# Opening stage of a one-core fp32 decoder layer: q, k and v blocks taken in pairs with seven quarter products, memory items moved ahead of them, and four residual additions moved in GpSimd's order at the end

## The chip, the cores and the metric

The kernel runs on one core of one Trainium2 chip, in one launch. The metric is device time in microseconds (us). Engines are named as in the profile: PE is the tensor engine's matmul (PEld its weight load), DVE the vector engine, ACT the scalar engine, POOL is GpSimd, SP is the engine that issues the DMAs.

## What is computed

One layer of a hybrid decoder for 1024 tokens of width 1024: a norm, one wide input projection, three token mixers (stick-breaking attention, an SSD scan, cross-attention to 256 memory tokens), their merge, and an MLP. The part that is changed is this:

```python
u = rms_norm(h, norm_mix_pre[layer])
proj = u @ w_in[layer]                      # 12320 columns
sb_qkv, z, xbc_raw, dt_raw, mem_q, gate_logits = jnp.split(proj, SPLIT_POINTS, axis=-1)
q, k, v = jnp.split(sb_qkv, 3, axis=-1)     # 1024 columns each
...
kv = rms_norm(mem, norm_mem) @ w_mem_kv     # 256 tokens, 2048 columns
...
ff = jnp.square(jax.nn.relu(u @ w_up[layer])) @ w_down[layer]
h = h + rms_norm(ff, norm_mlp_post[layer])
```

## The kernel before, in words

Every fp32 product is made of three passes. Each operand is rounded to fp32r ("hi") and the rest of it is kept ("lo"); `split3` names the passes hi*hi, hi*lo, lo*hi. So a block of 128 output columns for 1024 tokens, with an inner length of 1024, is 2 halves x 8 k-steps x 3 passes = 48 matmuls of 512 columns, and a memory item (128 columns, 256 memory tokens) is 24 matmuls of 256 columns.

`front` is the opening stage. Each of ten tiles (eight of x, two of mem) is squared and summed on ACT (`root_of`), scaled on DVE (`invert`), turned on PE (`turn`), multiplied by the gain on DVE from PSUM (`scale_turned`, result in `scaled`), rounded on ACT (`round_u`), and its rest taken on DVE (`rest_of_u`). Two weight blocks (b = 0, 1) are multiplied while the tiles come in, by `piece`, two tiles at a time. Then PE makes the projection of dt (48 matmuls, L464) and works through `ITEMS`: 22 further blocks of q (b < 8), k (b < 16) and v (b < 24), with the 16 memory items set between them. Weights come through a ring of three slots; POOL rounds them (L393) and takes their rest (L399). ACT evacuates each product, DVE takes the rest for q and k. Between blocks stand the small steps for dt, its running sums and their tables (L486 to L502, L547 to L559, L602 to L627).

`stick_breaking` follows in the same block of programs, with no barrier between. Its SP part begins with `early_loads`, called from inside `front`. Its PE program works in events. Event i first asks for score i, which needs ACT's `beta` of event i-1, then runs a share of filling matmuls (`project`, L822: x, z and mem_q blocks, 48 matmuls per block) and turns the weights of event i-2. ACT and DVE go through the same events in order. Block m = 0 is evacuated in halves (`evacuate`, L903), the first of them in event 1.

The MLP at the end, `mix_and_mlp`, already makes its up-projection (L2610) by seven quarter products for a pair of blocks: 7 x 4 k-steps x 3 passes = 84 matmuls instead of 96. The down-projection takes 112 items of 12 matmuls (L2709). For each item POOL makes a weight difference (L2500), ACT rounds weight and activation (L2874, L2882) and DVE takes both rests (L3207, L3212). POOL's list also holds four residual additions (L2565), each of which waits for DVE's `scale` (L3238) of an output tile.

Of the kernel before, what the change touches and what calls it, by code (L numbers as in the profile page):

```python
# [80 lines left out]
class FrontSignals:  # L81
    u_split: Any
    kv_out: Any
    hi_out: Any
    qk_stored: Any
    v_stored: Any
# [149 lines left out]
def front(nc, ctx, a, proj, qk, kv, decay, table, dt_out, xh, xl, consts):  # L236

    def sb(n, shape, dt=F32):
        return ctx.enter_context(nc.sbuf_tensor(f"fr_{n}", shape, dt))
# [4 lines left out]
    N_BLOCKS, N_QK, N_KV = Z0, V0, 2 * KB  # L244
    FIRST_KV = 5
    SLOTS = 3
    ITEMS = [("in", b) for b in range(FIRST_KV + 1)]
    for m in range(N_KV):
        ITEMS += [("kv", m), ("in", FIRST_KV + 1 + m)]
    ITEMS += [("in", b) for b in range(FIRST_KV + 1 + N_KV, N_BLOCKS)]  # L250
    TILES = TB + MB

    w_raw = sb("w", [P, SLOTS, D])
    w_hi, w_lo = sb("wh", [P, SLOTS, KB, P], F32R), sb("wl", [P, SLOTS, KB, P], F32R)
    v_tile = sb("v", [P, 2, S])
    memh, meml = sb("memh", [P, KB, M], F32R), sb("meml", [P, KB, M], F32R)
    x_tile, u, square = sb("x", [P, 4, D]), sb("u", [P, 2, D]), sb("sq", [P, D])
    scaled = sb("scaled", [P, 2, D])
    stats, gains, warm = sb("stats", [P, 3, TILES]), sb("gains", [P, 2, KB]), sb("warm", [P, 1])
    hi_tile, lo_tile = sb("hi", [P, 2, S], F32R), sb("lo", [P, 2, S], F32R)  # L260
    wd, wdh, wdl = sb("wd", [P, KB, 32]), sb("wdh", [P, KB, 32], F32R), sb("wdl", [P, KB, 32], F32R)
    bias_row, a_row = sb("bias", [P, 32]), sb("a", [P, 32])
    raw, capped, soft = (sb(n, [P, TB, 32]) for n in ("dtraw", "dtcap", "dtsoft"))
    ps = ctx.enter_context(nc.psum_tensor("fr_ps", [P, 2, S], F32))
    ps_misc = ctx.enter_context(nc.psum_tensor("fr_psm", [P, 4, HALF], F32))
    turned = [ps_misc[:, 2 * s:2 * s + 2].rearrange("p a n -> p (a n)") for s in range(2)]
    ps_dt = ps_misc[:, 0, 0:TB * 32].rearrange("p (t c) -> p t c", t=TB)
    ps_dtT = ps_misc[0:32, 1:3].rearrange("p a n -> p (a n)")
    ps_turned_sums = ps_dtT
    ps_cs = ps_misc[:, 3].rearrange("p (a n) -> p a n", a=2)  # L270
    ps_kv = [ps_misc[:, bank, 0:M] for bank in (0, 3)]
    dtT = sb("dtT", [32, S])
    da_out, sums = sb("da", [P, TB, SSD_HEADS]), sb("cs", [P, TB * SSD_HEADS])
    tables = sb("tables", [P, 3, TB * SSD_HEADS])
    sumsT, grownT = sb("csT", [32, S]), sb("grownT", [32, S])
    kv_tile = sb("kvout", [P, 2, M])
# [3253 lines left out]
```

## Time and profile before

| what | value |
|---|---|
| device time, median of 3 | 2713.86 us (2713.6 to 2715.26) |
| device time of the profiled execution | 2712.84 us |
| its span | 2711.1 us |
| granted clock, mean | 0.99 |
| PE busy | 2626.2 us, 97% of the span |
| DVE, ACT, POOL busy | 1707.7, 1124.3, 1384.2 us |
| last matmul of `front` starts | 356.10 us into the span |

PE is busy in 97% of the span, so what counts is the number of its matmuls and the few places where it stands still. Busy time of PE is modelled for pipelined matmuls: one matmul lasts longer than the distance to the next, so distances between starts are the better measure.

### The profile page before, as it was taken

Reading aid. Unit: us, or ns where it says so; the run is one execution under the profiler, and the core shown is the slowest. Engines: PE = TensorE matmul, PEld = TensorE weight load, DVE = VectorE, ACT = ScalarE, POOL = GpSimd, SP = SyncE. Lnnn points to the kernel's source line nnn. Section 1 sums busy time; section 2 is a strip of 40 time slices with the busy share of each in tenths; the row PEclk is TensorE's granted clock in tenths of the full one; section 3 lists DMA queues with packets and bytes.
Section 4 is the critical chain, followed back from the end, with each engine's and each line's share of the span. In section 5 each row is a group of like instructions: output and inputs, shape, how many; then the busy total and the mean of one; then the engine's idle time right before and its main releaser. Section 6 shows DMA issues by size and latency. Waiting matters only on the chain. (4 is left out here: it accounts for less than half of the span.)

```text
span 2711.1 us, 35282 instructions
## 1 busy us (share of the span) xinstructions
PE 2626.2 (97%) x12884; PEld 2199.2 (81%) x12884; DVE 1707.7 (63%) x1899; ACT 1124.3 (41%) x2001; POOL 1384.2 (51%) x831
## 2 busy tenths in 40 slices
PE   7999999999999999799999999999999999999998
PEld 6888888888888888688888777878887788888886
DVE  6100046776777677488888756663358877768567
ACT  4111034444444444466666554443144222244443
POOL 3466634545554554378887832545500666535224
PEclk9999999999999999899999999999999999999999
DMA  4344424243433332366676653444331344376573
GB/s 150 140 169 160 149 95 123 93 132 109 114 112 104 114 94 94 119 183 193 197 208 202 218 207 128 156 147 140 132 124 55 144 163 156 135 241 211 203 252 142
DMA packets 205994, 407.32 MB, mean 150 GB/s; under 512 B 19585, under 2 KB 100097, under 8 KB 205825
## 3 DMA queue, kind: packets, MB, share of 16 engines
q1 hardware_dynamic: 205824, 405.08, 45.3%
q8 instruction: 105, 1.72, 0.3%
q14 instruction: 65, 0.52, 0.1%
HBM read 286.91 MB, written 118.10 MB: 149 GB/s over the span
## 5 line engine op out<-in xcount | busy, mean ns | idle before, releaser
L989 POOL TENSOR_TENSOR sb_beta<-sb_beta,sb_rest 128x128 f32<-128x128 f32 (+7 forms) x128 | 164.1, 1282 | 388.9 <-DVE sb_rest L1049 388.9
L822 PE MATMUL sb_psg<-uh,sb_wl 128*128 128x512 f32 x768 | 309.9, 403 | 0.0
L822 PE MATMUL sb_psg<-ul,sb_wh 128*128 128x512 f32 x768 | 305.2, 397 | 0.0
L822 PE MATMUL sb_psg<-uh,sb_wh 128*128 128x512 f32 x768 | 303.7, 395 | 0.0
L2709 PE MATMUL ff_ps<-ff_mh,ff_total 128*128 128x512 f32 x896 | 279.3, 392 | 5.6 <-DVE ff_total L3212 5.6
L1049 DVE TENSOR_TENSOR_SCAN sb_rest<-sb_rest 128x128 f32<-128x128 f32 (+7 forms) x128 | 185.2, 1447 | 151.1 <-ACT sb_rest L938 150.9
L2709 PEld LDWEIGHTS ff_ps<-ff_mh,ff_total 128*128 128x128 f32 x896 | 169.6, 189 | 42.7 <-issue 7.1
L1854 PE MATMUL first_ps<-uh,mg_wh 128*128 128x512 f32 x480 | 192.8, 402 | 7.4 <-DVE ul L2059 4.9
L1854 PE MATMUL first_ps<-uh,mg_wl 128*128 128x512 f32 x480 | 187.7, 391 | 0.0
L1854 PE MATMUL first_ps<-ul,mg_wh 128*128 128x512 f32 x480 | 187.6, 391 | 0.0
L2709 PE MATMUL ff_ps<-ff_ml,ff_total 128*128 128x512 f32 x448 | 175.5, 392 | 0.0
L822 PEld LDWEIGHTS sb_psg<-ul,sb_wh 128*128 128x128 f32 x768 | 144.7, 188 | 29.7
L822 PEld LDWEIGHTS sb_psg<-uh,sb_wl 128*128 128x128 f32 x768 | 145.1, 189 | 25.9
L822 PEld LDWEIGHTS sb_psg<-uh,sb_wh 128*128 128x128 f32 x768 | 145.3, 189 | 24.8
L901 ACT ACTIVATE sb_wth<-sb_pst 128x512 fp32r<-128x512 f32 (+1 forms) x192 | 87.3, 489 | 187.6 <-PE sb_pst L807 187.6
L426 PE MATMUL fr_ps<-uh,fr_wh 128*128 128x512 f32 (+1 forms) x416 | 157.5, 379 | 6.7 <-DVE ul L583 6.7
L1341 PE MATMUL first_ps<-uh,sg_wh 128*128 128x512 f32 x384 | 154.2, 402 | 7.9 <-ACT ssd_out L1406 7.0
L426 PE MATMUL fr_ps<-ul,fr_wh 128*128 128x512 f32 (+1 forms) x416 | 156.2, 375 | 0.0
L426 PE MATMUL fr_ps<-uh,fr_wl 128*128 128x512 f32 (+1 forms) x416 | 155.9, 375 | 0.0
L1341 PE MATMUL first_ps<-ul,sg_wh 128*128 128x512 f32 x384 | 150.4, 392 | 0.0
L1341 PE MATMUL first_ps<-uh,sg_wl 128*128 128x512 f32 x384 | 150.4, 392 | 0.0
L997 DVE TENSOR_TENSOR sb_wtl<-sb_pst,sb_wth 128x512 fp32r<-128x512 f32 (+1 forms) x192 | 99.7, 547 | 74.2 <-ACT sb_wth L901 74.2
(378 smaller groups left out, 7120.0 us busy)
## 6 DMA issues: line engine op xcount, KB each, us to landing
sb_w<-in_w_in SPq DMA_DIRECT2D x48, 512.0 KB, 4.5
scratch_proj<-sb_out SPq DMA_DIRECT2D x48, 512.0 KB, 2.9
ff_w<-in_w_down SPq DMA_DIRECT2D x96, 256.0 KB, 3.6
sb_k<-scratch_qk SPq DMA_DIRECT2D x64, 256.0 KB, 6.3
ssd_arow<-scratch_decay SPq DMA_DIRECT2D x32, 512.0 KB, 5.6
mg_gate<-scratch_proj SPq DMA_DIRECT2D x32, 512.0 KB, 3.6
ff_w<-in_w_up SPq DMA_DIRECT2D x32, 512.0 KB, 3.8
mg_w<-in_w_branch SPq DMA_DIRECT2D x30, 512.0 KB, 4.3
```

What stands on the lines that cost most here:

```text
L426: last = nc.tensor.matmul(ps[:, b % 2, cols], l[:, s, k], r[:, k, cols], start=(k == 0 and j == 0), stop=(k == KB - 1 and j == 2))
L822: last = nc.tensor.matmul(ps_g[:, h], l[:, s, k], r[:, k, h * HALF:(h + 1) * HALF], start=(k == 0 and j == 0), stop=(k == KB - 1 and j == 2))
L901: nc.scalar.activation(out, src, ACT.Copy).then_inc(hi_done, 1)
L989: nc.gpsimd.tensor_tensor(beta[:, i % 3, 0:cols], beta[:, i % 3, 0:cols], rest[:, i % 3, 0:cols], ALU.mult).then_inc(weighted, 1)
L997: nc.vector.tensor_tensor(out, src, hi, ALU.subtract).then_inc(lo_done, 1)
L1049: nc.vector.tensor_tensor_scan(kept, kept, kept, 1.0, ALU.mult, ALU.bypass).then_inc(scanned, 1)
L1341: last = nc.tensor.matmul(ps_g[:, h], l[:, s, k], r[:, k, h * HALF:(h + 1) * HALF], start=(k == 0 and j == 0), stop=(k == KB - 1 and j == 2))
L1854: last = nc.tensor.matmul(ps[:, s, cols], l[:, k], r[:, k, cols], start=(k == 0 and j == 0), stop=(k == KB - 1 and j == 2))
L2709: done = nc.tensor.matmul(down_bank(p, local), l[:, columns(local)], r, start=(begins and c == 0 and j == 0), stop=(c == PAIRS - 1 and j = ...
```

## The change

`front` is rewritten. Blocks 0 and 1 stay as they are. The 16 memory items come next, one after another, and their weights are rounded by ACT and finished by DVE instead of by POOL. Then blocks 2 to 23 come as 11 pairs. A pair is treated as a 2x2 matrix of quarters (two row blocks, two halves of k) times a 2x2 matrix of u (two halves of k, two halves of the tokens), and is made by seven products of 12 matmuls (`p1`, `p5`, `p2`, `p6`, `p7`, `p4`, `p3`) with sums of weight quarters made by POOL (`weight_sums`) and sums of quarters of u (T1 to T4) made once by POOL and split by ACT and DVE during the memory items. T1 takes the place of the quarter B12 of u in `xh`, `xl`; B12 is stored to DRAM (`kept`) and loaded back at the end by `load_kept`. DVE adds up the outputs (`c11` to `c12`). `early_loads` has the new loads in it, and the two tiles of the last pair are stored after it. ACT's first `evacuate` in `stick_breaking` waits for all stores of `front` (`before.outs`). In the MLP the four residual additions stand at other items of POOL's list.

```diff
+        def near_sums(i):
+            j = i - TB // 2
+            pool.wait_ge(gained, i + 1)
+            pool.wait_ge(raw_kept, TB)
+            x = by_block(scaled[:, i % 2])
+            minus(T1_raw[:, :, columns(j)], x[:, LOWER], B11_raw[:, :, columns(j)]).then_inc(t_near, 1)
+            minus(T3_raw[:, :, columns(j)], x[:, UPPER], x[:, LOWER]).then_inc(t_near, 1)
...
-        for n in range(2, len(ITEMS)):
-            round_item(n)
-            rest_of_item(n)
+        for i in range(TB // 2, TB):
+            near_sums(i)
+        pool.wait_ge(t_near, TB)
+        nc.gpsimd.tensor_tensor(T2_raw, T3_raw, B11_raw, ALU.add).then_inc(t_far, 1)
+        pool.wait_ge(t_far, 1)
+        minus(T4_raw, T2_raw, B21_raw).then_inc(t_far, 1)
+        for c in range(PAIRS):
+            weight_sums(c)
...
+        def product(p, c, factor, moving):
+            for k in range(Q):
+                for j, (l, r) in enumerate(split3(*zip(factor, moving))):
+                    done = nc.tensor.matmul(bank(p, c), l[:, k * P:(k + 1) * P], r[:, k],
+                                            start=(k == 0 and j == 0), stop=(k == Q - 1 and j == 2))
+            done.then_inc(p_done[p], 1)
...
+        for m in range(N_KV):
+            product_of_memory(m)
+            if m == 2:
...
+            if m == 7:
                 pe.wait_ge(dt_dve, 5)
                 da_all = da_out[:].rearrange("p c h -> p (c h)")
...
+        for m in range(N_KV):
+            if 1 <= m <= 4:
+                round_t(m)
+            evacuate_kv(m)
+            if m + 3 < N_KV:
+                round_kv(m + 3)
+            if m == 5:
                 act.wait_ge(dt_dve, 2)
...
+            if m == 6:
                 dve.wait_ge(dt_act, 3)
...
     def early_loads(sp):
-        sp.wait_ge(before.u_split, TILES)
+        for signal, count in before.qk_outs:
+            sp.wait_ge(signal, count)
+        sp.wait_ge(before.p_done[6], before.pairs)
         load(sp, 0)
-        load_qk(sp, 0, 0)
+        load_q(sp, 0, 0)
         load(sp, 1)
+        sp.wait_ge(before.p_done[4], before.pairs)
+        load_k(sp, 0, 0)
+        before.load_kept(sp)
...
                 if m < 2:
-                    stored_before, blocks = ((before.kv_stored, KV_BLOCKS), (before.v_stored, V_BLOCKS))[m]
-                    for x in range(2):
-                        act.wait_ge(stored_before[x], 16 * blocks // 2)
+                    for signal, count in before.outs:
+                        act.wait_ge(signal, count)
...
+            else:
+                pool.wait_ge(before.p_done[7], before.pairs)
...
             for t in range(TB // 2):
-                if n == 6 * PAIRS + 5 + 3 * t:
+                if n == min(6 * PAIRS + 11 + 2 * t, N_DOWN - 1):
                     pool.wait_ge(scaled_done, t + 1)
```

POOL in the opening stage. Before, behind the two rests of the first weight blocks and the split of dt's weights, its list went on with the rounding and the rest of weight item 2, and so on for 38 items:

```order
L399 TENSOR_TENSOR fr_wl<-fr_w,fr_wh 128x1024 x2
L405 CAST fr_wdh<-fr_wd 128x256
L407 TENSOR_TENSOR fr_wdl<-fr_wd,fr_wdh 128x256
L393 TENSOR_TENSOR fr_wh<-fr_w,small 128x1024
L399 TENSOR_TENSOR fr_wl<-fr_w,fr_wh 128x1024
```

Now, at the same place, come the sums for the last four tiles of x (`fr_f_hi` is `scaled`, `fr_f_t` the raw T and B quarters), one pair of rows for each tile, and then the two long ones:

```order
L498 TENSOR_TENSOR fr_fl<-fr_w,fr_fh 128x1024 x2
L532 CAST fr_wdh<-fr_wd 128x256
L534 TENSOR_TENSOR fr_wdl<-fr_wd,fr_wdh 128x256
L494 TENSOR_TENSOR fr_f_t<-fr_f_hi,fr_f_t 128x4x128
L494 TENSOR_TENSOR fr_f_t<-fr_f_hi 128x4x128
...
L538 TENSOR_TENSOR fr_f_t<-fr_f_t 128x2048
L494 TENSOR_TENSOR fr_f_t<-fr_f_t 128x2048
L516 TENSOR_TENSOR fr_f_sums<-fr_w 128x512
```

No weight splitting is left in POOL's list; eight short and two long sums of u stand there, then four sums per pair.

SP at the hand-over from `front` to `stick_breaking`. Before, the early loads of `sb_` tiles followed the last memory item's store, while three v blocks were still to be made:

```order
L337 DMA scratch_kv<-fr_kvout 128x256
L742 DMA sb_w<-in_w_in 128x1024
L730 DMA sb_q<-scratch_qk 64x1024
L732 DMA sb_k<-scratch_qk 64x1024 x2
L730 DMA sb_q<-scratch_qk 64x1024
L732 DMA sb_k<-scratch_qk 64x1024 x2
L742 DMA sb_w<-in_w_in 128x1024
```

Now they begin after the sixth product of the last pair, and the store of the last two v blocks (L451, 512 KB each) is the last row:

```order
L1168 DMA sb_w<-in_w_in 128x1024
L1150 DMA sb_q<-scratch_qk 64x1024 x2
L1168 DMA sb_w<-in_w_in 128x1024
L1157 DMA sb_k<-scratch_qk 64x1024 x4
L1029 DMA uh<-scratch_kept 128x4x512
L1029 DMA ul<-scratch_kept 128x4x512
...
L1150 DMA sb_q<-scratch_qk 64x1024 x2
L1157 DMA sb_k<-scratch_qk 64x1024 x4
L1162 DMA sb_vraw<-scratch_proj 128x1024
L451 DMA scratch_proj<-fr_f_tiles 128x1024 x2
```

Two 1 MB loads have come in (`uh`, `ul`), and seventeen transfers now stand ahead of the last stores of v, besides two small ones (conv weights).

POOL at the end of the MLP, last group of items. `ff_f_vh` are the output tiles. Before:

```order
L2500 TENSOR_TENSOR ff_f_vl<-ff_w,ff_f_vl 128x512 x6
L2565 TENSOR_TENSOR ff_f_vh<-ff_f_vh,ff_f_near 128x1024
L2500 TENSOR_TENSOR ff_f_vl<-ff_w,ff_f_vl 128x512 x3
L2565 TENSOR_TENSOR ff_f_vh<-ff_f_vh,ff_f_near 128x1024
L2500 TENSOR_TENSOR ff_f_vl<-ff_w,ff_f_vl 128x512 x3
```

Now:

```order
L2948 TENSOR_TENSOR ff_f_vl<-ff_w,ff_f_vl 128x512 x12
L3013 TENSOR_TENSOR ff_f_vh<-ff_f_vh,ff_f_near 128x1024
L2948 TENSOR_TENSOR ff_f_vl<-ff_w,ff_f_vl 128x512 x2
L3013 TENSOR_TENSOR ff_f_vh<-ff_f_vh,ff_f_near 128x1024
L2948 TENSOR_TENSOR ff_f_vl<-ff_w,ff_f_vl 128x512 x2
L3013 TENSOR_TENSOR ff_f_vh<-ff_f_vh,ff_f_near 128x1024 x2
```

Twelve weight differences instead of six stand ahead of the first addition, and no difference is left behind the third.

## Rows read from the trace of the kernel before

**Rows 1.** A window of the opening stage: busy us of each engine, clock, DMA share, GB/s.

```profile
150.00:200.00 50.00, 50.00 (x267) 43.34 (x266) 4.90 (x4) 5.41 (x8) 32.86 (x16) 1.00 0.46 159
```

**Rows 2.** Timeline of PE in the opening stage: start, duration, line, tiles.

```profile
262.04 0.39 PE L426 MATMUL fr_ps<-uh,fr_wl 128*128 128x512 f32 x1
...
265.44 0.39 PE L426 MATMUL fr_ps<-uh,fr_wl 128*128 128x512 f32 x1
265.67 0.28 PE L442 MATMUL fr_psm<-fr_memh,fr_wh 128*128 128x256 f32 x1
...
268.42 0.28 PE L442 MATMUL fr_psm<-fr_memh,fr_wl 128*128 128x256 f32 x1
```

**Rows 3.** Window of the MLP's up-projection, columns as in rows 1.

```profile
2160.00:2180.00 20.00, 20.00 (x90) 16.57 (x89) 16.73 (x21) 4.60 (x7) 13.55 (x10) 1.00 0.48 178
```

**Rows 4.** Timeline of DVE, one tile of the opening norm.

```profile
46.56 1.22 DVE L577 TENSOR_TENSOR fr_scaled<-fr_psm,fr_gains 128x1024 f32<-128x1024 f32 x1
48.91 1.23 DVE L583 TENSOR_TENSOR ul<-fr_scaled,uh 128x1024 fp32r<-128x1024 f32 x1 [1.13 <-ACT uh L515]
...
50.24 0.76 DVE L568 TENSOR_SCALAR fr_u<-fr_x,fr_stats 128x1024 f32<-128x1024 f32 x1
50.91 1.22 DVE L577 TENSOR_TENSOR fr_scaled<-fr_psm,fr_gains 128x1024 f32<-128x1024 f32 x1
```

**Rows 5.** Timeline, a POOL and a DVE instruction at the same time.

```profile
56.32 2.42 POOL L399 TENSOR_TENSOR fr_wl<-fr_w,fr_wh 128x1024 fp32r<-128x1024 f32 x1
...
56.75 3.07 DVE L583 TENSOR_TENSOR fr_meml<-fr_scaled,fr_memh 128x1024 fp32r<-128x1024 f32 x1 [1.13 <-ACT fr_memh L515]
```

**Rows 6.** The tile of the dt projection: ns min/median/max, first and last start.

```profile
L464 PE MATMUL fr_psm<-uh,fr_wdh x16: 387/390/397, 56.9 to 67.2; 128*32 128x512 f32 x16
```

**Rows 7.** Timeline of POOL, a difference of 512 columns.

```profile
2213.07 1.29 POOL L2509 TENSOR_TENSOR ff_f_total<-ff_w 128x512 f32<-128x512 f32 x1 [0.72 <-DVE ff_total L3143]
```

**Rows 8.** Groups of ACT by line: busy, mean ns, idle before.

```profile
L515 ACT ACTIVATE uh<-fr_scaled 128x1024 fp32r<-128x1024 f32 x8 | 8.5, 1057 | 15.6 <-DVE fr_scaled L577 15.6
L524 ACT ACTIVATE fr_kvout<-fr_psm 128x256 f32<-128x256 f32 x16 | 6.1, 384 | 28.6 <-PE fr_psm L442 28.6
```

**Rows 9.** Timeline of ACT, the step for dt.

```profile
83.65 0.42 ACT L549 ACTIVATE fr_dtsoft<-fr_dtcap 128x256 f32<-128x256 f32 x1 [2.34 <-DVE fr_dtcap L611]
...
85.91 1.28 ACT L552 ACT_TABLE_LOAD   x1
87.20 0.23 ACT L552 ACTIVATE fr_a<-fr_a 128x32 f32<-128x32 f32 x1
```

**Rows 10.** DMA issues of the page: count, KB each, median us to landing.

```profile
sb_w<-in_w_in SPq DMA_DIRECT2D x48, 512.0 KB, 4.5
```

**Rows 11.** Timeline at the hand-over: PE, then ACT.

```profile
356.32 0.39 PE L822 MATMUL sb_psg<-uh,sb_wh 128*128 128x512 f32 x1
...
366.34 0.60 ACT L918 ACTIVATE sb_padded<-sb_psg 128x512 f32<-128x512 f32 x1 [3.52 <-PE sb_psg L822]
...
367.21 0.50 ACT L942 ACTIVATE sb_beta<-sb_psz 128x384 f32<-128x384 f32 x1
...
370.95 0.60 ACT L938 ACTIVATE sb_rest<-sb_psz 128x512 f32<-128x512 f32 x1 [2.15 <-PE sb_psz L843]
```

**Rows 12.** Windows around the hand-over, columns as in rows 1.

```profile
324.00:346.00 22.00, 22.00 (x99) 18.20 (x98) 1.37 (x4) 1.63 (x3) 10.01 (x5) 1.00 1.03 264
...
360.00:364.00 4.00, 2.87 (x8) 2.44 (x9) 1.85 (x2) 1.73 (x5) 2.30 (x2) 0.65 0.33 117
```

**Rows 13.** Waits from 2560 us on: us in total, times, longest.

```profile
PE ff_ps L2709 <- DVE ff_total L3212: 5.6, 4, 2.6
```

**Rows 14.** Timeline of PE and POOL in the last items.

```profile
2670.34 0.47 PE L2709 MATMUL ff_ps<-ff_mh,ff_total 128*128 128x512 f32 x1 [0.67 <-DVE ff_total L3212]
...
2675.90 2.73 POOL L2565 TENSOR_TENSOR ff_f_vh<-ff_f_vh,ff_f_near 128x1024 f32<-128x1024 f32 x1 [1.16 <-DVE ff_f_vh L3238]
...
2703.40 0.39 PE L2709 MATMUL ff_ps<-ff_mh,ff_total 128*128 128x512 f32 x1
```

More of the change, by code:

```diff
@@ L81 @@
 class FrontSignals:
[L82 to L86, printed above, removed]
+    pairs: Any
+    p_done: Any
+    raw_used: Any
+    bank_free: Any
+    qk_outs: Any
+    outs: Any
+    stored_at: Any
+    load_kept: Any
+    b12_back: Any
     kv_stored: Any
@@ L233, in product, with front @@
     return last
-def front(nc, ctx, a, proj, qk, kv, decay, table, dt_out, xh, xl, consts):
-    def sb(n, shape, dt=F32):
-        return ctx.enter_context(nc.sbuf_tensor(f"fr_{n}", shape, dt))
+def front(nc, ctx, a, proj, qk, kv, decay, table, dt_out, kept, xh, xl, consts):
     def sem(n):
         return nc.alloc_semaphore(f"fr_{n}")
[L244 to L276, printed above, removed]
@@ new lines, in front, with small @@
+    with ExitStack() as plain_view:
+        plain = layout(plain_view, "f_", F32)
+    held = layout(ctx, "", F32R)
+    def small(n, shape, dt=F32):
+        return ctx.enter_context(nc.sbuf_tensor(f"fr_{n}", shape, dt))
+    raw, fh, fl, hi_tiles = held["w"], held["fh"], held["fl"], held["hi"]
+    tiles, tiles_low = plain["tiles"], held["tiles"]
+    p1_kept = held["p1"]
+    sums = [plain["sums"][:, x // 2, (x % 2) * HALF:(x % 2 + 1) * HALF] for x in range(4)]
+    first_low = held["sums"]
@@ new lines, in front @@
+    back_hi, back_lo = ([held["back"][:, 2 * x + y] for x in range(BACK)] for y in range(2))
+    x_tile = plain["back"][:, 0:8].rearrange("p (s a) n -> p s (a n)", a=2)
+    square = plain["back"][:, 8:10].rearrange("p a n -> p (a n)")
+    third_hi, third_lo = (held["back"][:, x:x + 2].rearrange("p a n -> p (a n)") for x in (6, 8))
+    u, scaled = plain["sums"], plain["hi"]
+    memh, meml = (held["tiles"][:, x:x + 2].rearrange("p a n -> p (a n)").rearrange("p (k m) -> p k m", k=KB) for x in (0, 2))
@@ L420, in turn, with piece @@
             last.then_inc(turned_done, 1)
-        def piece(n, cols):
-            s, b = n % SLOTS, ITEMS[n][1]
+        def piece(b, cols):
+            half = cols.start // HALF
+            out = acc[:, 2 * b + half, cols.start - half * HALF:cols.stop - half * HALF]
             for k in range(KB):
-                for j, (l, r) in enumerate(split3((w_hi, xh), (w_lo, xl))):
-                    last = nc.tensor.matmul(ps[:, b % 2, cols], l[:, s, k], r[:, k, cols],
+                for j, (l, r) in enumerate(split3((fh, xh), (fl, xl))):
+                    last = nc.tensor.matmul(out, l[:, b, k * P:(k + 1) * P], r[:, k, cols],
@@ new lines, in vector @@
+            if m == 14:
+                rest_of_front(0)
+        for which in (S1, S2, S3, A22, S4):
+            rest_of_back(which, 0)
+        for c in range(PAIRS):
+            more = c + 1 < PAIRS
+            if c and is_split(c - 1):
+                for row in range(2):
+                    lo_of_tile(c - 1, row)
+            if more:
+                rest_of_front(c + 1)
+                rest_of_back(S1, c + 1)
+            c11(c)
+            make_u2(c)
+            if more:
+                rest_of_back(S2, c + 1)
+            make_u3(c)
+            make_u4(c)
+            c22(c)
+            if more:
+                rest_of_back(S3, c + 1)
+            c21(c)
+            if more:
+                rest_of_back(A22, c + 1)
+            c12(c)
+            if more:
+                rest_of_back(S4, c + 1)
@@ L730, in load_qk, with load_k @@
             sp.dma_start(q_both[to, a].bitcast(F32), qk[half, p + Q0, rows]).then_inc(qk_loaded[a], 16)
+    def load_k(sp, p, a):
+        rows = slice(64 * a, 64 * a + 64)
+        for half in range(2):
+            to = slice(64 * half, 64 * half + 64)
             for part in range(2):
```

654 lines of the change are left out of this document (493 added, 161 removed).

## The prediction

> **What bounds the kernel now.** I read the windows first. In the opening stage PE is busy 50.00 of 50 us at full clock, while DVE and ACT work about a tenth of the time [rows 1]. So from the dt projection to the end of `front` only PE's own work counts, and every matmul taken away is time, as long as what feeds PE keeps up. The price of a matmul comes from distances between starts: 15 matmuls of 512 columns lie between 262.04 and 265.44, or 0.2267 us each; 23 matmuls of 256 columns lie between 265.67 and 268.42, or 0.12 us each [rows 2]. In the norm of the tiles ahead of it the tiles follow each other at a fixed distance of 50.91 - 46.56 = 4.35 us. That is a loop through two engines: DVE scales (1.22), ACT rounds (DVE waits 1.13 for it), DVE takes the rest (1.23), then makes the next tile's `fr_u` (0.76, behind a reciprocal) and scales again [rows 4]. At the end of the MLP PE waits four times for DVE, 5.6 us in all [rows 13].
>
> **Term 1, the matmuls.** Eleven pairs at 84 instead of 96 matmuls are 132 fewer. At 0.2267 us that is **-29.9 us**. Whether PE can run at that pace in this form shows in the MLP's up-projection, which has the same seven products per pair: 20.00 of 20 us busy at full clock, DVE at 16.73 and POOL at 13.55 [rows 3]. A pair takes 84 x 0.2267 = 19.0 us there and here. The new pairs ask for less: ACT about 7 us (copies of 512 and 1024 columns at 0.6 and 1.06 [rows 8, 11]), DVE some 12 rests and sums of 512 columns and three rests of 1024 at 1.23 [rows 4], about 11 us, POOL four sums at 1.29 [rows 7], 5 us. That work I cost at nothing; it lies beside the pair's 19.0 us of PE, and without that cover the longest of it, DVE's, would add up to 11 us per pair.
>
> **Term 2, the norm of the tiles.** POOL gets two sums of 512 columns per tile for the last four x tiles, then two of 2048. DVE and POOL can't both work on SBUF operands: POOL's instruction runs from 56.32 to 58.74, and DVE's rest, ready at 56.75, ends at 59.82, its own 1.1 us behind POOL's end [rows 5]. The first short sum (1.29) hides behind ACT's 1.13. The second falls between DVE's rest and its next scaling, so the loop goes from 4.35 to about 5.6 us for three distances: +3.8. The extra copies on ACT in the early tiles cost little (+0.8 at the first piece), and POOL no longer splits item 2 there (-1.3). So the scaling of tile 7, before at 46.56 [rows 4], comes at about 49.9. One loop of 5.6 on, tile 8 is scaled at 55.5 to 56.7, and at the same moment POOL begins its first sum of 2048 columns, four times 1.29 less overheads, say 4.9, until 60.4. ACT has rounded tile 8 at 57.8; DVE's rest of it waits for POOL and ends at 61.6, and the scaling of tile 9 at 62.8. The dt projection waits for that one and begins at 62.9 instead of 56.8 [rows 6]: **+6.1 us** (low 2.5, if the short sums hide wholly; high 9, if the second long sum gets in ahead of DVE as well). The rest of tile 9, held by the second sum until 67.5, is hidden behind the dt projection's 10.9 us.
>
> **Term 3, the memory items in a row.** Sixteen items of 24 matmuls take 2.88 us each, as before. But each now also asks ACT for a rounding (1.06) and an evacuation (0.38) [rows 8], and DVE for a rest (1.23). During items 1 to 4 ACT and DVE also split T1 to T4, 2048 columns each: twice the 1.06 and twice the 1.23 for 1024, about 2.1 us on ACT and 2.4 on DVE. So ACT has 3.5 and DVE 3.6 us of work in 2.88; three items of lead take up most of it, about +0.9. The larger piece is dt. ACT's step from the first exponential to the last takes 83.65 to 87.43, and a table load like the one at 85.91 (1.28 us) goes ahead of it, so some 5 us [rows 9]. Behind it in ACT's list stand evacuation 6 and rounding 9, and only behind the rest of item 9 does DVE make `fr_da`, for which PE waits after item 7. From the end of product 5: evacuation and rounding 1.4, the wait for `capped` and the step to about 8.2, evacuation 6 and rounding 9 to 9.6, rest 9 (1.23) and three short DVE instructions for dt (together 0.9) to 12.1. PE arrives 2 x 2.88 after product 5, plus 0.9 that item 7 is late, at 6.7: PE stands for **5.4 us**. Before, a whole block of 10.9 us covered this step, and nothing was ahead of it on DVE. After a stop of 2 us the clock was granted at 0.65 over four us [rows 12], a loss of 1.4; for this one I take 2. Two smaller waits (for the running sums after item 10, 0.3; for the last evacuation ahead of pair 0, 0.5) make the term **+9.1 us** (low 1, if the dt step's table load is done in advance and ACT runs ahead; high 13).
>
> **Term 4, the hand-over.** Let T be the start of the last pair; its products end every 2.72 us, the seventh at T+19.0. The first `sb_w` is asked for at T+10.9 and lands 4.5 us later [rows 10]; POOL's rest takes up to 2.42 [rows 5] and its rounding somewhat less, together 4.3, so PE can begin at T+19.7: +0.7. Then comes the queue. Before, the same loads were asked for 30 us earlier. The transfers from `sb_w` to the stores of v are 5 x 0.52 MB (two weights, one v, two stores), 12 x 0.26 MB (q and k) and 2 x 1.05 MB (B12), 7.9 MB. The early loads ran at 264 GB/s with the DMA engines full [rows 12], so 7.9 MB take 30 us, and the stores, asked for last, are down at T+42. Score 0 needs its k (fifth to eighth transfer), at about T+24 instead of T+22.1: +1.9. ACT's first evacuation comes 10.0 us after the first matmul of the stage [rows 11], here at T+31.5, and stands for the stores until T+42. Behind it in ACT's list are the sigmoids of event 2, and PE's score 3 waits for those. Before, ACT had finished them at 367.7 and stood 2.15 us of the 3.2 until 370.95 for score 3 [rows 11]; between the two I take 2.6 us that PE has in hand: 10.5 - 2.6 = 7.9. The clock after the stop: 2. Sum **+12.5 us** (low 1, high 16).
>
> Here a rule gives another result. By the Trainium skill (DMA: Bandwidth & Descriptors, "Where 436 GB/s comes from") it is the memory side that binds such transfers, at about 358 GB/s per core. An estimate by that page: 7.9 MB in 22 us, the stores down at T+35, k early enough, and a term of about 4 us. The row with 264 GB/s, more than half of it the same q and k loads, decides for me.
>
> The early loads and the stores may also not wait for one another as I assume; both ways the result is the first rival below.
>
> **Term 5, the end of the MLP.** Now POOL waits for `scale` at item 101 and stands; the sums behind come late, each addition takes 2.7 us in which DVE waits [rows 14]. From the first late item at 2670.34 to the last matmul at 2703.40 lie nine items of 12 matmuls, which at 0.2267 take 24.5 us; PE used 33.1, and it had waited 0.7 before the first. With 5.6 us of waits [rows 13] the rest is slow clock. After the change twelve sums stand ahead of the first addition, and DVE needs per item 2 x 0.6 and POOL 1.25, plus 0.6 for `scale`, 3.1 us against 2.72 for a few items, within a lead of five. **-9 us** (-5 if one addition still bites; no gain beyond 33.1 + 0.7 - 24.5 = 9.3 is there). The outputs 0 to 3 are then added some 5 us before PE ends, so their stores don't delay the last ones.
>
> **Sum.** -29.9 + 6.1 + 9.1 + 12.5 - 9.0 = -11.2 us, against a profiled execution of 2712.84 us (span 2711.1): 2701.6. The median of the runs is 1.0 above the profiled one, so **2702.6 us**. 0.2% of the time, 5.4 us, is about what a measurement can tell from no change.
>
> **Rivals.**
> - The hand-over is nearly free, because the queue drains at the faster rate or the stores don't stand behind the loads: by rows, if the 7.9 MB take no longer than the 20.5 us from T+11 to ACT's need at T+31.5 (385 GB/s), only the 0.7 and at most the 1.9 are left, and the time is 2692.7. For it: the two loads of B12 and the stores fill all partitions, unlike q and k (64 rows each). Against it: the DMA engines stood at a share of 1.03 for 22 us in the early loads [rows 12]. Chance 0.2.
> - The memory items cost more: each of the four splits of T pushes ACT and DVE further behind, and the stop for dt costs the full clock penalty twice; term 3 at 15 to 17 and term 2 at 9 give 2709 to 2713, no change that can be told. ACT's 3.5 and DVE's 3.6 us against 2.88 speak for it, the lead of three slots against it. Chance 0.13.
> - Slower: the pairs starve. SP's list has the stores of pair c, which wait for ACT's and DVE's split of its tiles in the next pair, ahead of the next weight loads, and POOL's sums wait for both weights of a pair. I find some 9 us in hand for the last factor of a pair. If a round took that and 2.8 us more over ten pairs (28 us), the time would be 2730; from 0.6 us per pair on the change is no longer faster by more than 0.2%, from 1.7 on it is slower by more than that. Against it: the same order of products with busier engines loses nothing in the MLP [rows 3]. Chance 0.1.
> - The forecast as it stands, 2697 to 2707: 0.47. The rest, 0.1, is the forecast with term 5 or term 1 smaller by some us.
>
> **How the numbers follow.** The range 2690 to 2711 takes in the free hand-over and most of the second rival, and leaves out the starving pairs. Faster by over 0.2% are the forecast, the free hand-over and most of the rest: 0.77. Within 0.2%: the second rival: 0.13. Slower: 0.10.
>
> **What the changed profile would show.** Right: PE 50 of 50 us through the pairs, 19.0 us between the first products of two pairs; the dt projection about 6 us later; one stop of PE of about 5 us in the memory items ahead of the running sums' matmuls, and a lower clock behind it; ACT's first `sb_padded` waiting for a store for about 10 us, PE standing for about 8 in the same place; no PE wait in the last 16 items. It would be wrong if the pairs showed PE waiting for rests, if the dt stop were covered, or if the stores of v landed before T+32.

## The result, and the profile after the change

The changed kernel takes **2720.35 us** (median of 13 runs, 2715.24 to 2722.59) against 2714.03 us of the kernel before on the same chip: ratio **1.0022**, 95% interval 1.0014 to 1.0029. It is slower by about 6 us, where 11 us less were forecast; the time lies outside the range. The profiled execution took 2720.81 us (span 2719.1), 8.0 us more than that of the kernel before.

I first followed the loss by places that both programs have, with their times in the two traces:

| place | before, us | after, us | difference |
|---|---|---|---|
| PE starts the dt projection | 56.9 | 59.2 | +2.3 |
| PE starts the projections of the next stage (`sb_psg`) | 356.3 | 353.7 | -2.6 |
| PE starts the second block of these projections (their 49th matmul) | 373.0 | 382.0 | +9.0 |
| PE starts the projections of the stage after it | 1136.2 | 1147.9 | +11.7 |
| PE starts the MLP's up-projection | 2088.7 | 2100.0 | +11.3 |
| PE starts the down-projection | 2389.4 | 2400.7 | +11.3 |
| PE starts its last matmul | 2703.4 | 2711.4 | +8.0 |

So the opening stage gains 4.9 us behind the dt projection, the hand-over loses 11.6 within its first block of projections, another 2.7 come between its last block and the stage after it, and the end of the MLP returns 3.3. (The 2.7 and the 3.3 can be the spread of single traces, as the section on the prediction shows.) The first of these is the surprise: with 29.9 us of matmuls taken out and 9.8 put on (the forecast's 9.1 for the memory items and the 0.7 of the hand-over that falls ahead of `sb_psg`), it should be 20.

The waits of PE up to 430 us in the changed kernel (total in us, times, longest):

```profile
PE fr_ps L582 <- DVE fr_f_tiles L930: 9.3, 5, 2.2
PE sb_psz L1289 <- ACT sb_beta L1387: 7.7, 2, 5.9
...
PE fr_ps L675 <- DVE fr_da L985: 4.7, 1, 4.7
PE sb_psz L1289 <- DMA sb_k<-scratch_qk: 1.8, 1, 1.8
```

The second, third and fourth stops had been forecast. The first had not: L582 is the matmul of the pairs, and five times it waits for DVE's c22 of the pair before. The windows over the pairs (columns as in rows 1) show the same as lost PE time, where all but the first, which begins ahead of pair 0, should be full:

```profile
129.00:160.00 31.00, 30.65 (x135) 25.44 (x136) 17.45 (x22) 10.54 (x16) 6.93 (x5) 1.00 0.38 133
160.00:190.00 30.00, 30.00 (x134) 24.82 (x134) 14.54 (x20) 9.73 (x15) 11.16 (x8) 1.00 0.36 133
190.00:220.00 30.00, 27.75 (x122) 22.34 (x121) 19.26 (x27) 9.87 (x13) 5.59 (x4) 1.00 0.35 133
220.00:250.00 30.00, 27.75 (x115) 22.28 (x114) 12.19 (x16) 6.50 (x10) 6.88 (x5) 0.94 0.48 183
250.00:280.00 30.00, 27.39 (x120) 22.05 (x119) 18.26 (x26) 10.03 (x15) 9.89 (x7) 1.00 0.28 105
280.00:310.00 30.00, 27.78 (x115) 22.33 (x114) 13.88 (x19) 7.44 (x10) 6.73 (x5) 0.94 0.46 175
```

None of the engines that feed PE is full: DVE works 12 to 19 us of 30, ACT 7 to 11, POOL 6 to 11, the DMA engines 0.28 to 0.48 of the time. It is not a lack of throughput but a chain. From the start of pair 0 at 129.35 to `sb_psg` at 353.7 PE takes 224.3 us for eleven pairs of 19.05: **14.8 us lost**, 9.3 in waits, 3.6 in slow clock (two windows of 30 us at 0.94) and 1.9 around them, of which 0.3 fall at the hand-over itself. DVE's c22 comes every 21.6 to 21.8 us (191.3, 212.9, 234.7, 256.5), and every 21.5 on average from 170.2 to 299.2.

One such round, engine by engine. SP stores the split tiles of a pair and only then asks for the next two weights:

```profile
197.95 0.46 SPq L447 DMA_DIRECT2D scratch_qk<-fr_tiles  x1
198.51 2.28 SPq L415 DMA_DIRECT2D fr_w<-in_w_in  x2
217.18 0.33 SPq L445 DMA_DIRECT2D scratch_qk<-fr_hi  x1
...
219.58 0.46 SPq L447 DMA_DIRECT2D scratch_qk<-fr_tiles  x1
220.14 2.31 SPq L415 DMA_DIRECT2D fr_w<-in_w_in  x2
```

GpSimd's sums wait for both weights; it had been idle for 15.9 us:

```profile
205.15 1.29 POOL L516 TENSOR_TENSOR fr_f_sums<-fr_w 128x512 f32<-128x512 f32 x1 [15.88 <-issue]
```

DVE's list, from the rest of S1 over c22 (L930) and c12 (L943) to the rests of the tiles:

```profile
207.14 1.23 DVE L898 TENSOR_TENSOR fr_back<-fr_f_sums,fr_back 128x512 fp32r<-128x512 f32 x1 [8.08 <-ACT fr_back L771]
...
210.99 0.69 DVE L898 TENSOR_TENSOR fr_back<-fr_f_sums,fr_back 128x512 fp32r<-128x512 f32 x1 [1.43 <-POOL fr_f_sums L494]
...
212.93 0.68 DVE L930 TENSOR_TENSOR fr_f_tiles<-fr_ps,fr_f_tiles 128x512 f32<-128x512 f32 x1
...
215.33 0.69 DVE L943 TENSOR_TENSOR fr_f_tiles<-fr_ps,fr_f_tiles 128x512 f32<-128x512 f32 x1
...
217.19 2.36 DVE L948 TENSOR_TENSOR fr_tiles<-fr_f_tiles,fr_hi 128x1024 fp32r<-128x1024 f32 x2 [0.58 <-ACT fr_hi L792]
```

And PE, which had finished the pair's last product at 205.8, stands at p2 of the next pair:

```profile
213.67 0.50 PE L582 MATMUL fr_ps<-uh,fr_fh 128*128 128x512 f32 x1 [2.25 <-DVE fr_f_tiles L930]
```

Read in a circle: load asked for at 198.51, sums from 205.15 (6.6 us), the rest of S2 behind the fourth sum at 211 (5.8), then u3, u4, c22, c21 and c12 with rests between them to 216.0 (5.0), the tiles' split and stores to 220.14 (4.1), next load. 21.6 us against PE's 19.05.

The same trace holds rows that speak for this reading. The circle passes through the split of the tiles, and only q and k tiles are split; of the eleven pairs the last four are v. From there on the stores (L451) wait for no split, and c22 comes every 17.3 to 17.4 us, so DVE makes up what it was behind and PE waits no more. So it is the stores of the seven q and k pairs that starve PE; its last such stop ends at 299.9. SP's list there, and c22:

```profile
302.37 0.80 SPq L451 DMA_DIRECT2D scratch_proj<-fr_f_tiles  x2
303.26 1.85 SPq L415 DMA_DIRECT2D fr_w<-in_w_in  x2
319.79 0.80 SPq L451 DMA_DIRECT2D scratch_proj<-fr_f_tiles  x2
```

```profile
316.64 0.68 DVE L930 TENSOR_TENSOR fr_f_tiles<-fr_ps,fr_f_tiles 128x512 f32<-128x512 f32 x1
...
333.97 0.68 DVE L930 TENSOR_TENSOR fr_f_tiles<-fr_ps,fr_f_tiles 128x512 f32<-128x512 f32 x1
```

### The profile page after: what moved, and what is told of

Same layout as the page of the kernel before. It is cut to its first block and busy times, and to the rows that moved or that the text cites. A ratio compares the mean times of both kernels' runs of the same rounds, so it can differ in the third digit from the quotient of the medians.

```text
span 2719.1 us, 35512 instructions
## 1 busy us (share of the span) xinstructions
PE 2610.4 (96%) x12752; PEld 2182.6 (80%) x12752; DVE 1830.0 (67%) x2062; ACT 1191.9 (44%) x2098; POOL 1308.9 (48%) x809
## 5 line engine op out<-in xcount | busy, mean ns | idle before, releaser
L1267 PE MATMUL sb_psg<-uh,sb_wl 128*128 128x512 f32 x768 | 311.4, 406 | 0.0
L1267 PE MATMUL sb_psg<-ul,sb_wh 128*128 128x512 f32 x768 | 305.9, 398 | 0.0
L1267 PE MATMUL sb_psg<-uh,sb_wh 128*128 128x512 f32 x768 | 304.6, 397 | 0.1
L1267 PEld LDWEIGHTS sb_psg<-ul,sb_wh 128*128 128x128 f32 x768 | 145.4, 189 | 30.3
L1267 PEld LDWEIGHTS sb_psg<-uh,sb_wl 128*128 128x128 f32 x768 | 145.8, 190 | 25.8
L1267 PEld LDWEIGHTS sb_psg<-uh,sb_wh 128*128 128x128 f32 x768 | 146.1, 190 | 24.8 <-POOL sb_wl L1422 0.6
L1789 PE MATMUL first_ps<-uh,ssd_gwh 128*128 128x512 f32 x384 | 154.0, 401 | 7.9 <-ACT ssd_out L1854 6.9
L1789 PE MATMUL first_ps<-uh,ssd_gwl 128*128 128x512 f32 x384 | 150.4, 392 | 0.0
L1789 PE MATMUL first_ps<-ul,ssd_gwh 128*128 128x512 f32 x384 | 150.4, 392 | 0.0
L2280 POOL TENSOR_TENSOR merged<-merged,mg_gate 128x1024 f32<-128x1024 f32 x24 | 60.3, 2514 | 158.9 <-DVE mg_gate L2514 158.9
L1461 DVE SCALAR_TENSOR_TENSOR sb_out<-sb_padded,sb_cw,sb_out 128x1024 f32<-128x1024 f32 x72 | 131.7, 1829 | 1.7
L1383 ACT ACTIVATE sb_rest<-sb_psz 128x128 f32<-128x128 f32 (+7 forms) x128 | 83.6, 653 | 110.7 <-PE sb_psz L1289 109.8
```

The costliest lines, as they stand in the source:

```text
L1267: last = nc.tensor.matmul(ps_g[:, h], l[:, s, k], r[:, k, h * HALF:(h + 1) * HALF], start=(k == 0 and j == 0), stop=(k == KB - 1 and j == 2))
L1383: nc.scalar.activation(rest[:, i % 3, 1:cols + 1], ps_z[:, 0:cols], ACT.Sigmoid, scale=-0.125).then_inc(keep_done, 1)
L1461: nc.vector.scalar_tensor_tensor(out_tile[:, 0], padded[:, tap:tap + S], cw[:, n, tap:tap + 1], out_tile[:, 0], ALU.mult, ALU.add).then_in ...
L1789: last = nc.tensor.matmul(ps_g[:, h], l[:, s, k], r[:, k, h * HALF:(h + 1) * HALF], start=(k == 0 and j == 0), stop=(k == KB - 1 and j == 2))
```

## Experiments

Times are medians and ratios are to the kernel before, which took 2714.93 us beside e1 to e4, 2714.36 beside e5 to e7 and 2714.00 beside e8 and e9. The changed kernel was not run beside them; differences to it are to its 2720.35, and with intervals of 0.1% on each side they are good to some 3 us.

**e1, additions back at the old places.**

```
-                if n == min(6 * PAIRS + 11 + 2 * t, N_DOWN - 1):
+                if n == 6 * PAIRS + 5 + 3 * t:
```

> The changed kernel with GpSimd's additions of the residual put back to the old places in its list; nothing else differs. What the trace of the changed kernel shows (the down products start 11.3 us later than before, the last one ends 8.0 us later): the new places bring 3.3 us, so this kernel should take 3.3 us more, about 2723.7, with PE waiting 5.6 us for DVE in the last 16 items as before. What the prediction had: they bring 9 us, 2729. If the places bring nothing: 2720.4.

2722.17 us (ratio 1.0025, 1.0015 to 1.0036): 1.8 us more, PE's waits in the last items 5.3 us against 3.6. So the new places bring some 2 us, which is less than these runs can tell from nothing, and not 9. This run also shows how far two traces of one program differ: its opening stages are those of the changed kernel, and it starts the stage after the hand-over's at 1143.3 instead of 1147.9.

**e2, weight loads ahead of the stores.**

```
             for n in (item_of(c, 0) + 3, item_of(c, 0) + 4):
                 if n < item_of(PAIRS, 0):
                     load_item(n)
-            if c < PAIRS - 1:
-                store_pair(c)
+            if c:
+                store_pair(c - 1)
```

> In SP's list of the pairs the two weight loads of a round come ahead of the stores of the pair before, instead of the stores of the same pair ahead of the next loads. Theory A (the pairs starve in a loop: a store waits for ACT's and DVE's split of the tile, the next weight load is queued behind it, GpSimd's sums wait for the load, the splits of the next pair for the sums): the period of a pair falls from 21.6 to 19.05 us, PE's waits for DVE's c22 (9.3 us in five pairs) are gone, the project stage starts about 14 us earlier, the time is about 2706. Rival B (the order in DVE's and ACT's lists or the lock between DVE and GpSimd sets the period): loads land earlier, PE waits remain, the time stays within 3 us of 2720. Rival C (the 14 us are won and lost again at the hand-over, since its transfers are the limit): 2715 or more.

**2708.41 us**, ratio 0.9972 (0.9962 to 0.9982), now faster than before. The windows over the pairs:

```profile
190.00:220.00 30.00, 30.00 (x134) 24.85 (x133) 19.36 (x24) 10.54 (x15) 6.76 (x6) 1.00 0.52 193
220.00:250.00 30.00, 30.00 (x134) 24.86 (x133) 19.76 (x25) 11.71 (x16) 8.76 (x7) 1.00 0.39 146
250.00:280.00 30.00, 30.00 (x134) 24.82 (x134) 19.95 (x26) 8.38 (x12) 9.04 (x7) 1.00 0.45 170
```

PE 30.00 of 30, as in every window from 129 to 334; c22 comes every 19.0 us, and `sb_psg` starts at 338.4, 15.3 us earlier than in the changed kernel. The same instructions in the same order on PE, DVE, ACT and GpSimd run at PE's pace; only SP's list differs. Rival B falls. By the medians 11.9 us of the 15.3 reach the end. Nothing is lost at the hand-over as rival C had it: from `sb_psg` to the next stage this run takes 794.6 us and the changed kernel 794.2. (The trace of e2 is that of the slowest of its nine runs, 2713.09 us; from the stage behind the hand-over's to the MLP it takes 6.7 us more than that of the changed kernel for the same instructions, so the end is to be read from the medians.)

**e3, the last pair's stores early.** SP's list at the hand-over:

```
-        early_loads(sp)
-        store_pair(PAIRS - 1)
+        early_loads(sp, lambda: store_pair(PAIRS - 1))
...
         before.load_kept(sp)
+        store_last()
         sp.wait_ge(before.tables_stored, 16 * (1 + 2 * GROUPS))
```

> At the hand-over the stores of the last pair's two tiles stand in SP's list behind the first weights, the first q and k and the two halves of B12, ahead of the other loads (they stood last). Theory A (ACT's first sb_padded waits 12.7 us for the last store and PE's scores wait behind it): the store lands some 8 us earlier, PE stands 5 to 8 us less between 360 and 380 us, the time is about 2713. Rival B (what is late is the load of the convolution's constants and k, which this order puts later still by the stores): no gain or a loss of up to 3 us, 2720 to 2723.

**2715.0 us**, ratio 1.0002 (0.9993 to 1.0011), 5.4 less. In the changed kernel SP asks for the two stores at 360.24, and ACT's first evacuation, with the sigmoids of the next scores behind it, waits 12.7 us for them:

```profile
360.24 0.84 SPq L451 DMA_DIRECT2D scratch_proj<-fr_f_tiles  x2
```

```profile
375.08 0.60 ACT L1363 ACTIVATE sb_padded<-sb_psg 128x512 f32<-128x512 f32 x1 [12.69 <-DMA scratch_proj<-fr_f_tiles]
```

```profile
358.26 0.33 PE L1289 MATMUL sb_psz<-sb_k,sb_q 128*128 128x128 f32 x1 [1.77 <-DMA sb_k<-scratch_qk]
360.68 0.58 PE L1289 MATMUL sb_psz<-sb_k,sb_q 128*128 128x256 f32 x1 [1.87 <-ACT sb_beta L1387]
376.49 0.79 PE L1289 MATMUL sb_psz<-sb_k,sb_q 128*128 128x512 f32 x1 [5.87 <-ACT sb_beta L1387]
```

In e3 the stores are asked for at 352.91, and the same evacuation waits only for PE:

```profile
365.19 0.60 ACT L1363 ACTIVATE sb_padded<-sb_psg 128x512 f32<-128x512 f32 x1 [4.70 <-PE sb_psg L1267]
```

The third of PE's waits is gone. The first block of projections behind the hand-over takes 19.9 us from `sb_psg` on, where it takes 28.3 in the changed kernel, 28.6 in e1, 28.9 in e2 and 16.7 before the change. So 8.4 of the 11.6 us were this one wait and the slow clock behind it, by the traces; by the medians 5.4. The expectation of a loss from later constants did not come true.

**e4, the running sums of dt two items later.** On PE, and alike for what follows on DVE and ACT:

```
-            if m == 7:
+            if m == 9:
                 pe.wait_ge(dt_dve, 5)
```

> The running sums of dt are taken by PE after memory item 9 instead of 7, and what follows them two items later each. Theory A (PE stands 4.7 us for fr_da, because ACT's exponential and logarithm and two other items stand ahead of it, and loses some clock behind the stop): the stop is gone, pair 0 starts 5 to 6 us earlier, 2715. Rival B (ACT's rounding of the items is itself late behind the dt step, so that the next product waits for its item where PE would have waited for fr_da): the wait moves to an item's product, the gain is 2 us or less, 2718 to 2720.

**2714.96 us**, ratio 1.0006 (0.9996 to 1.0015), 5.4 less. The wait for `fr_da` is gone; PE waits 2.6 us for `fr_kvout` and 1.9 for `fr_fl` instead of 0.8 and 1.0, and pair 0 starts at 124.8 instead of 129.35. The intervals of the two kernels just touch; e5 shows the gain again. What PE waited for in the changed kernel shows on ACT. It loads the tables of its functions three times, 1.28 us each:

```profile
91.58 1.28 ACT L815 ACT_TABLE_LOAD   x1
93.11 0.42 ACT L815 ACTIVATE fr_dtsoft<-fr_dtcap 128x256 f32<-128x256 f32 x1 [0.25 <-DVE fr_dtcap L979]
93.55 1.28 ACT L817 ACT_TABLE_LOAD   x1
...
95.37 1.28 ACT L818 ACT_TABLE_LOAD   x1
...
98.27 1.06 ACT L727 ACTIVATE fr_fh<-fr_w 128x1024 fp32r<-128x1024 f32 x1
```

DVE's rests for it end in `fr_da` at 99.82, and PE goes on at 100.31:

```profile
100.31 1.22 PE L675 MATMUL fr_ps<-fr_da,tri 128*128 128x256 f32 x2 [4.70 <-DVE fr_da L985]
```

The granted clock behind that stop (windows, columns as in rows 1) is 0.50 for four us and 0.81 for six:

```profile
100.00:104.00 4.00, 3.69 (x13) 3.34 (x14) 1.39 (x2) 0.00 (x0) 0.00 (x0) 0.50 0.67 231
104.00:110.00 6.00, 6.00 (x44) 6.00 (x44) 1.22 (x1) 1.38 (x3) 0.00 (x0) 0.81 0.23 70
```

**e5, the edits of e2, e3 and e4 together.**

> The three edits together: weight loads ahead of the stores of the pair before, the last pair's stores ahead of the later loads at the hand-over, the running sums of dt two memory items later. If they are three separate losses, their gains add: 11.9 + 5.4 + 5.4 = 22.7 us against the changed kernel by the medians so far, 2698. Rival (the hand-over is bound by its transfers, so that what comes earlier ahead of it is lost there): the pairs' and dt's gains shrink to half, 2706.

**2696.34 us**, ratio 0.9939 (0.9927 to 0.9952): 18.0 us faster than before, 24 faster than the changed kernel. The three gains add (11.9 + 5.4 + 5.4 = 22.7), within what can be told, so none of the losses hides another.

**e6, the residual added by DVE,** on top of e5: GpSimd's four additions go, and behind DVE's scaling of a tile stands

```
+            dve.wait_ge(scaled_done, t + 1)
+            dve.wait_ge(h_back, 16 * TB)
+            nc.vector.tensor_tensor(out_tiles[:, t], out_tiles[:, t], h_tiles[t], ALU.add).then_inc(finished, 1)
```

> As the run with the three edits, and the residual of the first four output tiles is added by DVE directly behind its scaling (one more instruction of about 1.2 us each) instead of by GpSimd (2.85 us each, in which DVE stands). Theory A (it is the time in which GpSimd and DVE exclude each other that makes PE wait at the end of the MLP, wherever the additions stand in GpSimd's list): PE's waits of 4 to 5 us in the last 16 items go nearly to zero, and the time falls by 6 to 9 us. Rival B (DVE's own work per item is too much there, so the additions cost the same on DVE): waits as before, gain below 2 us.

**2691.12 us**, ratio 0.9922 (0.9909 to 0.9936), 5.2 less than e5 and the fastest kernel of the study. PE's waits in the last items (e5, then e6):

```profile
PE ff_ps L3157 <- DVE ff_total L3660: 6.1, 3, 3.3
```

```profile
PE ff_ps L3152 <- DVE ff_total L3655: 3.3, 3, 1.5
```

The waits halve and do not vanish; the gain is under the 6 to 9 of theory A, and over B's 2. The two intervals overlap a little, and e7, which has the same additions, is only 3.1 us under e5, so the gain is 3 to 5 us; the direction agrees with the waits. What is left has a cause of the same kind: GpSimd's weight differences run beside DVE's rests too, and in e6 some of these take 1.78 us instead of 0.68. e6 takes GpSimd's own work and its waits for `scale` out of its list as well; that these were not what PE waited for is read from the changed kernel, where DVE is busy 9.96 of every 10 us from 2660 to 2700, and was not tested by itself. In the changed kernel the additions and what DVE does under them are (timeline, GpSimd and then DVE):

```profile
2694.24 5.67 POOL L3013 TENSOR_TENSOR ff_f_vh<-ff_f_vh,ff_f_near 128x1024 f32<-128x1024 f32 x2
```

```profile
2692.45 0.68 DVE L3655 TENSOR_TENSOR ff_ml<-ff_f_vl,ff_mh 128x512 fp32r<-128x512 f32 x1
...
2694.76 2.89 DVE L3655 TENSOR_TENSOR ff_ml<-ff_f_vl,ff_mh 128x512 fp32r<-128x512 f32 x1
2697.57 2.88 DVE L3660 TENSOR_TENSOR ff_total<-ff_f_total,ff_total 128x512 fp32r<-128x512 f32 x1
```

A rest of 0.68 us takes 2.89 under an addition.

**e7, the convolution's constants ahead of B12,** on top of e6: the two small loads move in front of `load_kept`.

> As the run with the additions on DVE, and the convolution's constants (60 KB) are loaded ahead of the two halves of B12 (2.1 MB) instead of behind them. DVE's first scan waits for them from about 354.5 to 364 us in the changed kernel. If that wait is what ends PE's stop at the hand-over once the stores are early: DVE's scan starts some 5 us earlier and the time falls by 2 to 4 us. Rival (it is ACT's evacuation or the k load that PE waits for): no difference above 1 us.

2693.24 us (0.9925, 0.9913 to 0.9938): no gain; the 2.1 us more are inside the spread. DVE's first scan starts at 343.7 instead of 347.5, though `sb_psg` starts 2.4 us later in this run (337.2 instead of 334.8), and PE's waits there are the same 1.4 for k and 1.9 for ACT. The rival holds: PE's waits do not depend on that scan.

**e8, only DVE's order changed,** SP's list as in the changed kernel:

```
             c22(c)
+            c21(c)
+            c12(c)
             if more:
                 rest_of_back(S3, c + 1)
-            c21(c)
-            if more:
                 rest_of_back(A22, c + 1)
-            c12(c)
-            if more:
                 rest_of_back(S4, c + 1)
```

> The changed kernel with one other edit: in DVE's list c21 and c12 of a pair stand ahead of the rests of S3 and A22 of the next pair; SP's list is untouched. If the starving is a loop that runs from the weight load through GpSimd's sums, the splits, DVE's c22, c21 and c12, the tile's split and its store back to the next load, two rests of 0.6 us fewer lie on it: its period falls from 21.6 to about 20.4 us and the project stage starts some 5 to 8 us earlier, while PE waits in pairs remain. If the loop runs only through the store and the loads (the transfers themselves), the period stays 21.6 us.

2716.16 us (1.0007, 0.9996 to 1.0018), 4.2 less, with intervals that overlap a little. The starts of c22 in the starving pairs go from 172.0 to 296.5 in six rounds, 20.75 us each, against 21.5 in the changed kernel (170.2 to 299.2) and 19.0 in e2. PE still waits for c22, 6.5 us in five times, and `sb_psg` starts at 350.8, 2.9 us earlier and not the 5 to 8 expected. DVE's c12 lies on the loop, as the theory has it; but two rests off it bring 0.75 us a round, not 1.2. Where the other 0.45 stays I did not follow.

**e9, the kernel before with the additions at the new places** (the one-line edit of e1, the other way round).

> The kernel before with only GpSimd's additions of the residual at the new places. The prediction had 9 us for this alone. The pair of runs of the changed kernel with new and old places gives 1.8 us by the medians, 3.3 us by the two traces, so the theory that the exclusion of DVE is only moved to later items expects 2712 to 2714; the prediction 2706.

2711.87 us against 2714.00, ratio 0.9999 (0.9990 to 1.0007); PE waits 5.1 us there instead of 5.6 [rows 13]. No gain that can be measured.

## Why the prediction was wrong

**The step that failed is the sentence on the cover of term 1**: "That work I cost at nothing; it lies beside the pair's 19.0 us of PE." I had added the instructions of each engine and compared each sum with 19.0. That is the condition of throughput, and it holds: DVE, ACT and GpSimd have time over. What counts as well is the time once around the loop that SP's list closes, and that is 21.6 us. It cost 14.5 us by the trace (the 14.8 without the 0.3 at the hand-over), 11.9 by the median of e2. The rival "slower" named this mechanism and its place, and the loss, 1.5 us a pair if spread over its ten pairs, lies between its two thresholds of 0.6 and 1.7. In fact the loop is too long only in the seven q and k pairs. I gave it 0.1, with two arguments that were both poor. The "some 9 us in hand for the last factor of a pair" were a slack at one product, not the length of a round trip. And that the MLP loses nothing at [rows 3] shows only that such products can run: loads stand behind stores in SP's list there too, but those stores wait for sums of their own pair and for no split of a tile in the next one. The pieces of the loop lay open: a load of 4.5 us [rows 10], four sums at 1.29 [rows 7], eight sums and rests of DVE at half of 1.23 [rows 4], ACT's first rounding of a tile at 1.06 [rows 8] and DVE's two rests at 1.23. That is 4.5 + 5.2 + 4.9 + 1.1 + 2.5 = 18.2 us, less than one below PE's 19.05; two loads behind four stores, 6.6 us instead of 4.5, and the steps between engines take it past.

**Term 1 itself was right.** In e2 a pair takes 19.04 us, as 84 x 0.2267 says.

**Term 2, +6.1, measured +2.3.** The loop of a tile with GpSimd's short sums is 5.26 us (47.04 to 52.30) where I had 5.6, and tile 7, which I expected to be scaled at 49.9, was at 47.04, because the tiles ahead of the sums ran earlier than I had them. From there to the dt projection it took 12.2 us; the forecast had 13.0. The long sum from 51.91 met DVE's rest of tile 8, as forecast:

```profile
51.91 4.95 POOL L538 TENSOR_TENSOR fr_f_t<-fr_f_t 128x2048 f32<-128x2048 f32 x1
```

```profile
54.64 3.30 DVE L865 TENSOR_TENSOR fr_tiles<-fr_f_hi,fr_tiles 128x1024 fp32r<-128x1024 f32 x1 [1.13 <-ACT fr_tiles L706]
```

The mechanism (a rest of 1.23 becomes 3.3 under GpSimd's sum) and its place were right, its time 3 us too late.

**Term 3, +9.1, measured +10.2** (between the dt projection and `sb_psg` the trace has -4.9; that plus 29.9 of matmuls, less the 14.8 lost between pair 0 and `sb_psg`). The stop for dt was 4.7 us (5.4 forecast), at the place and for the reason given; e4, without it, is 5.4 us faster.

**Term 4, +12.5, measured about +11.9**: 0.3 ahead of `sb_psg` (0.7 forecast), and 11.6 in the first block of projections behind it, which took 28.3 us instead of 16.7. The second block opens here (L1267 over 381 to 383 us; first and last start at the end of the row):

```profile
L1267 PE MATMUL sb_psg<-uh,sb_wh x1: 628/628/628, 382.0 to 382.0; 128*128 128x512 f32 x1
```

From there to the last block both kernels take 724.0 us, so nothing more is lost. ACT was let go at 375.08, 40.5 us after the last pair's start at 334.6; the forecast had T+42. PE's long wait was 5.9 where I had 7.9, with more clock lost around it: 0.81 granted over the 36 us from 354 on, against 0.95 over the 36 from 356 on before the change. The first rival, a nearly free hand-over, is out. The rule that stood beside it does not decide it either: by the Trainium skill (DMA: Bandwidth & Descriptors, "Where 436 GB/s comes from") transfers between HBM and SBUF are bound at about 358 GB/s per core. Here they ran at two rates, both off that figure, as the last section shows.

**Term 5, -9.0, measured -3.3 in the trace, -1.8 by e1 and none that can be told by e9.** Even the 3.3 is hardly more than spread: from the first down product to the last matmul the seven traces with the additions at the new places and on GpSimd take 310.7 to 313.7 us, the two with the old places 312.4 and 314.0. I took PE's 5.6 us of waits for a matter of where the additions stand. They are a matter of what the additions do to DVE: each one holds it for about 2.2 us (2.89 against 0.68), and DVE has no such reserve in the last items. Moving them moves the stop. In the changed kernel it is here, PE busy 6.95 and DVE 9.96 of 10 us:

```profile
2680.00:2690.00 10.00, 6.95 (x29) 4.86 (x27) 9.96 (x8) 2.30 (x4) 8.79 (x5) 1.00 0.25 85
```

Moving them to the engine that suffered brings 3 to 5 us (e6, e7).

**The sum again, by the trace:** -29.9 (right), +14.5 (missing), +2.3, +10.2, +11.9, -3.3 make +5.7. Another 2.7 us come between the last block of projections and the next stage, and -0.4 between there and the MLP, together the 8.0 by which the spans differ. With the missing term taken out (e2) the kernel is 6.5 us faster than before; the forecast's -11.2 with term 5 at -3.3 would have been -5.5. That these two agree so well is in part luck: with terms 2 to 4 as measured too it is -8.8.

What stays open: single traces differ where nothing was changed. From the second block of projections to the last all eleven take 723.8 to 724.6 us, but from the last to the next stage 37.8 to 41.9 (the changed kernel 41.9, e1 38.2, before the change 39.1), and from there to the MLP 838.7 to 845.4 in those with the new `front`. So e3 and e4 are both 12 us ahead of the changed kernel where the stage after the hand-over's starts, but 5.4 us at the end by the medians. I put the 2.7 us and this difference down to that spread and did not test it.

## What to carry to other kernels

Work that is hidden beside the bound engine has to fit twice: its sum per round into the round, and every closed chain through the queues, once around, into it as well. Write the chain out whenever a load stands behind a store in one in-order list, because the store waits for the end of the round and the load is wanted at its beginning; here swapping two lines of SP's list was worth 12 us. And when one engine slows another by running beside it, a change of place moves the stop, while a change of engine removes part of it.
